# First column of x: half of it loaded in two parts by two queues, the first weights' high part made by VectorE, and two products put ahead of the second half's transposes

## What is computed

```python
h = rmsnorm(x, g_pre_mix)
proj = h @ w_in + b_in                     # 18 tiles of 128 columns
out_a = mixer_a(...)                       # sliding window, 8 query heads, 2 key heads
out_b = mixer_b(...)                       # chunked attention, 8 heads
x = x + rmsnorm(concat(out_a, out_b) @ w_out, g_post_mix)
u = square(relu(rmsnorm(x, g_pre_mlp) @ w_up))      # 1024 x 4096
x = x + rmsnorm(u @ w_down, g_post_mlp)
```

## Time and profile before

| | us |
|---|---|
| median of three runs | 1034.25 |
| the profiled execution | 1034.96 |
| its span, first to last instruction | 1032.9 |
| TensorE busy in the span | 1024.1 (99%) |
| VectorE | 771.6 (75%) |
| ScalarE | 470.1 (46%) |
| GpSimd | 220.3 (21%) |

### The profile page before, as it was taken

How to read it: one execution, slowest core, us unless ns; L and a number is a source line. 1 busy time by engine, 2 the same in 40 slices (tenths; PEclk the granted TensorE clock), 3 DMA queues, 4 the chain that set the end, 5 groups by cost and what they waited for, 6 DMA issues and landing times.

```text
span 1032.9 us, 15795 instructions
## 1 busy us (share of the span) xinstructions
PE 1024.1 (99%) x5525; PEld 852.3 (83%) x5525; DVE 771.6 (75%) x1507; ACT 470.1 (46%) x977; POOL 220.3 (21%) x218
## 2 busy tenths in 40 slices
PE   9999999999999999999999999999999999999997
PEld 8899887788777888888888888888888888888886
DVE  4955677766688478888988788786444777778997
ACT  6622355545478567836221221311344445454552
POOL 5200000000000003148675674771100000000000
PEclk9999999999999999999999999999999999999999
DMA  9935442110071474035444434446777733454344
GB/s 196 225 100 135 108 133 76 44 47 27 21 224 43 123 185 157 25 138 209 168 170 162 163 133 153 163 143 217 252 237 243 233 101 94 142 194 142 94 139 166
DMA packets 135070, 147.91 MB, mean 143 GB/s; under 512 B 72248, under 2 KB 85440, under 8 KB 132944
## 3 DMA queue, kind: packets, MB, share of 16 engines
q1 hardware_dynamic: 133920, 146.68, 45.7%
q10 hardware_dynamic: 688, 0.20, 0.1%
q0 software_dynamic: 384, 0.04, 0.1%
HBM read 103.65 MB, written 47.49 MB: 146 GB/s over the span
## 4 chain that ended last, share of the span: by engine, by line
PE 93%; DVE 3%; issue 2%; DMA 1%; ACT 1%; POOL 0%; DVEq 0%; SPq 0%; ACTq 0%
PE ps L2246 27%; PE ps L2248 27%; PE ps L2247 27%; PE ps L2469 3%; PE ps L2455 3%; PE ps L2436 2%; PE ps L2380 1%; DVE wc_lo L1922 1%; PE ps L2415 1%; PE ps L2590 1%; PE ps L2588 1%; PE ps L2576 1%; DMA up_raw<-in_w_up 1%; DVE b_lo L1911 1%; DMA xraw<-in_x 0%
## 5 line engine op out<-in xcount | busy, mean ns | idle before, releaser
L2246 PE MATMUL ps<-b_hi,wc_hi 128*128 128x512 f32 x448 | 174.8, 390 | 0.5 <-DVE wc_lo L1922 0.5
L2246 PE MATMUL ps<-tm_hi,sm_hi 128*128 128x512 f32 (+1 forms) x450 | 174.9, 389 | 0.0
L2247 PE MATMUL ps<-tm_lo,sm_hi 128*128 128x512 f32 (+1 forms) x450 | 174.8, 389 | 0.0
L2248 PE MATMUL ps<-tm_hi,sm_lo 128*128 128x512 f32 (+1 forms) x450 | 174.8, 389 | 0.0
L2247 PE MATMUL ps<-b_lo,wc_hi 128*128 128x512 f32 x448 | 174.5, 390 | 0.0
L2248 PE MATMUL ps<-b_hi,wc_lo 128*128 128x512 f32 x448 | 174.5, 390 | 0.0
L1484 ACT ACTIVATE sm_hi<-sm_raw 128x512 fp32r<-128x512 f32 x112 | 70.7, 631 | 163.0 <-DMA sm_raw<-u_matrices 163.0
L2150 DVE TENSOR_TENSOR sm_lo<-sm_raw,sm_hi 128x512 fp32r<-128x512 f32 x112 | 77.9, 695 | 78.1 <-ACT sm_hi L1484 77.4
L2246 PEld LDWEIGHTS ps<-b_hi,wc_hi 128*128 128x128 f32 x448 | 84.2, 188 | 18.4 <-DVE wc_lo L1922 0.9
L2248 PEld LDWEIGHTS ps<-tm_hi,sm_lo 128*128 128x128 f32 x450 | 84.5, 188 | 17.5
L2246 PEld LDWEIGHTS ps<-tm_hi,sm_hi 128*128 128x128 f32 x450 | 84.5, 188 | 17.3
(11 more groups left out here) (261 smaller groups left out, 2066.6 us busy)
## 6 DMA issues: line engine op xcount, KB each, us to landing
u_matrices<-stage SPq DMA_DIRECT2D x112, 256.0 KB, 2.0
sm_raw<-u_matrices SPq DMA_DIRECT2D x112, 256.0 KB, 2.6
up_raw<-in_w_up SPq DMA_DIRECT2D x16, 1024.0 KB, 5.0
w<-in_w_down SPq DMA_DIRECT2D x64, 256.0 KB, 3.8
w_raw<-in_w_in SPq DMA_DIRECT2D x8, 512.0 KB, 3.6
xr<-in_x SPq DMA_DIRECT2D x8, 512.0 KB, 4.5
x_rows<-xr SPq DMA_DIRECT2D x8, 512.0 KB, 4.8
xf<-x_rows SPq DMA_DIRECT2D x8, 512.0 KB, 3.6
```

Of the source, the lines that this page charges most:

```text
L2246: pe.matmul(out, w_hi_, x_hi_, start=start, stop=False)
L2247: pe.matmul(out, w_hi_, x_lo_, start=False, stop=False)
L2248: return pe.matmul(out, w_lo_, x_hi_, start=False, stop=stop)
```

## The change

What it does, part by part:

1. The first half of column 0 is loaded by two DMAs: SyncE loads tokens 0 to 255 in the place of the old load, and ScalarE loads tokens 256 to 511 ahead of its three weight loads. Both add to `s_in[0]`, so the waits for that semaphore ask for 32 instead of 16.
2. VectorE makes w1_hi of column 0, with a copy ahead of everything else it does for the columns; ScalarE no longer does.
3. TensorE multiplies ones six times instead of seven.
4. TensorE's order becomes: transposes of the first half, three turns, the products e = 2 and e = 1 of the first half, the transposes of the second half (with their wait for `s_x0`), product e = 0, and on as before.

```diff
@@ load_x
-                    sp.dma_start(xraw[:, 0, 0:4], src[:, 0:4]).then_inc(s_in[0], 16)
+                    sp.dma_start(xraw[:, 0, 0:2], src[:, 0:2]).then_inc(s_in[0], 16)
                     sp.dma_start(g1, g_pre_mix).then_inc(s_g1, 16)
                     sp.dma_start(xraw[:, 0, 4:8], src[:, 4:8]).then_inc(s_x0, 16)
@@ scalar
+            act.dma_start(xraw[:, 0, 2:4], x[2 * P:4 * P, 0:P].rearrange("(t p) n -> p t n", p=P)).then_inc(s_in[0], 16)
             load_first_weights(act, 0)
...
-                        act.wait_ge(s_in[k], 16)
+                        act.wait_ge(s_in[k], 16 if k else 32)
...
-                        if k == 0 and h == 0:
-                            first_hi(0)
@@ vector
+            dve.wait_ge(s_w1[0], 48)
+            nc.vector.tensor_copy(w1_hi[:, 0], w1_raw[:, 0]).then_inc(s_w1hi, 1)
             dve.wait_ge(s_g1, 16)
@@ tensor
+            def first_transposes(h):
+                pe.wait_ge(*((s_x0, 16) if h else (s_in[0], 32)))
+                for t in range(h * (T // 2), (h + 1) * (T // 2)):
+                    last = pe.transpose(two(0)[:, t * P:(t + 1) * P], xraw[:, 0, t], ident[:])
+                last.then_inc(s_xt, 1)
...
-            keep_awake(7)
+            keep_awake(6)
             pe.wait_ge(s_id, 3)
-            x_transposes(0)
-
+            first_transposes(0)
+            turns(3)
             pe.wait_ge(s_xhi, 1)
             pe.wait_ge(s_w1hi, 1)
             for e in (2, 1, 0):
                 if e == 0:
+                    first_transposes(1)
                     pe.wait_ge(s_xlo, 1)
```

More of the change, by code:

```diff
@@ L1199, in wo_high @@
             def wo_high(k):
-                act.wait_ge(s_in[k], (64 if k in EXCHANGED else 16) + (32 if k < 4 else 16))
+                act.wait_ge(s_in[k], (64 if k in EXCHANGED else 16 if k else 32) + (32 if k < 4 else 16))
                 nc.scalar.activation(wo_hi[:, k], wo_raw[:, k], ACT.Copy).then_inc(s_wohi, 1)
@@ L2254, in x_transposes @@
                 for t in range(T):
[L2255 to L2258, removed]
+                    last = pe.transpose(two(6)[:, t * P:(t + 1) * P], xraw[:, k, t], ident[:])
                     if k < 2 and t == T // 2 - 1:
```

## The result

| | before | after |
|---|---|---|
| median of 6 runs, us | 1034.53 (1034.15 to 1034.73) | 1037.9 (1036.75 to 1038.98) |
| profiled execution | 1034.96 | 1038.98 |
| its span | 1032.9 | 1037.2 |

The ratio is 1.0035, with a 95% interval of 1.0024 to 1.0046: slower by some 3.5 us, where I had forecast 1034.2 and no change that can be told. The result lies outside my range of 1033.6 to 1035.9. The runs also lie further apart, over 2.2 us in place of 0.6. The profiled execution of the changed kernel is the slowest of its six, so what its trace shows is a bad case of the loss and not the middle one.

The account below looks back on a forecast made before the run. TensorE, busy 99% of the span, was taken as the bound; 1034.96 less a 0.1 us gain gives 1034.86, and the median lying 0.71 us below that execution gives 1034.15, rounded 1034.2; range 1033.6 to 1035.9.

Parts of the forecast that it names:

- the weights' high part: Column 0's w_hi on VectorE: third weight load lands at 5.28, copy ready for TensorE at 5.85, at no cost.
- the weights land last: Rival: weights landing at 6.4 hold the first products until 6.97; 0.47 us lost, 1034.7; chance 0.12.
- The clock: Rival at TensorE's start: gaps delay the rise past 7.13, up to 2.4 us lost (1036.6), around 1035.5 if partial; chance 0.18.
- The two rivals: Late weights before the first products (0.47 us, chance 0.12) and a later clock rise (up to 2.4 us, chance 0.18).
- the forecast gain: At product e = 0 of column 0: start at 7.36 instead of 7.44, a gain of 0.1 us.
- One pair of ones fewer: At TensorE's start: frees it 0.49 us earlier, at 3.71 instead of 4.20; no gain by itself.
- The order: Two products before the second half's transposes: same 1.71 us of lower-level work before e = 0, waits in between met.
- Transposes at 3.94: First half's transposes on TensorE were to start at 3.90 instead of 4.29, just behind the landing.
- the half landed: First half of column 0, loaded in two parts: 3.1 us to landing, at 3.85 instead of 4.16.
- the copy: VectorE's w_hi copy of 384 elements in SBUF: 0.42 us, ending at 5.75.
- product e = 0: Last first-half product of column 0 on TensorE: start at 7.36, with bounds of 7.29 or 7.56.

Follow-up runs that it names:

- e6: The changed kernel with SyncE holding back column 1 and all later loads until the first weights have landed; 1036.53 us in one run.
- e2: The changed kernel without the load in two parts: the first half is one SyncE load again; 1034.38 us.
- e11: The changed kernel with the second half's transposes put back ahead of all products; 1036.47 us.
- e1: The kernel before with only the load of the first half in two parts added; 1036.27 us.
- e8: The changed kernel with one weight load moved to SyncE's queue, ahead of g1 and the second half, and six turns instead of three; 1034.74 us.
- e8b: The same kernel as e8, run again for its comparison with the kernel before; 1034.78 us.
- e5: The kernel before without the multiplications of ones and the three turns, whose results are unused; 1036.41 us.
- e9: The kernel of e8 with the second half's transposes ahead of all products, as in the kernel before; 1034.6 us.
- e10: The kernel of e2 with seven pairs of ones instead of six and five turns instead of three; 1034.65 us.
- e7: The changed kernel with its weight loads reordered, the two in 256-byte pieces first and the one in 512-byte pieces last; 1037.02 us.

## Why the prediction was wrong

**The step that failed is the weights' high part**, and in it the duration of the third weight load. I took 3.1 us for it, from the row of the kernel before, and bounded it by 2.5 and 4.24. Both bounds came from loads issued before column 1's 512 KB. The load took 5.45 us in the profile, and 4.3 to 5.45 in the four profiled executions that have the change's loads. The issue moved by 0.6 us (to 2.30, forecast 2.18), the landing by 2.3 us more than that, and the first product by 2.4 us against the forecast (8.28 for 5.88). e6 points to the cause that was left out of the bound: at 2.30 the load is issued behind column 1's 512 KB (2.24), and with those and the later loads held back it takes 3.5 us, in one execution. The rival "the weights land last" named the mechanism, with a price of 0.47 us from a bound that was too near and a chance of 0.12.

**The clock was priced as if it stood by itself.** I had it rise later because of small gaps, 0.18, for 1.5 to 2.4 us. The small gaps alone did little to the median: e2 has them and differs from the kernel before by 0.3 us, inside its interval. In the profile of the change the clock had already risen, by 4.4 us, and fell in the gap of 3.39 us that the late weights make. The length of the gaps alone does not tell: the clock also fell in e11, after gaps of 0.81 and 0.92 us, and stayed up in e1, after 1.14 and 0.47 us. The two rivals came together: wait 1.8 us, clock 2.7 us in the profiled execution. A bound on the first should have carried the price of the second.

The moment at which the clock rose before was read a little wrong as well. I let a first product at the lower level take 0.43 us. In the change, at a granted clock of 0.50, the first one takes 0.56 us to the second (8.28 to 8.84), and only the next ones 0.43. By that the clock rose at about 7.0, not at 7.13, and the forecast gain would have been 0.14 us in place of 0.1. One pair of ones fewer shortened their row by 0.43 us (3.36 to 2.93), not 0.49, as 14 matmuls have 13 spaces and not 12. Neither matters beside the weights.

**The order.** That w_hi is no longer covered by the transposes was said, at no cost. The cost can appear once the weights are late: the second half's transposes leave the wait, which is then one gap of 3.39 us instead of two shorter ones, and come after it, at the lower level (9.27 to 9.98). The profile of e2 shows this cost, 1.89 us at column 1 together with the late clock. The difference between e11 and the change, about 1.4 us, fits it, but its interval is too wide to call the share shown.

**What held.** Transposes at 3.94 (forecast 3.90); the half landed at 0.76 + 3.0 = 3.76 (3.85); the copy took 0.36 us (0.42); what TensorE lost at the head went through to the end of the span almost whole (4.3 of 4.54). The lower level doubles the spacing: the lo x hi products of the change stand 0.43 apart (three from 10.55 to 11.83), 0.23 at the upper level. In e8 and e8b, where the weights are in time, product e = 0 started at 7.21 and 6.93, for my 7.36, both helped by a clock that rose earlier, by the spacing at about 6.7 and before 4.3. That a view of the granted clock without an entry doesn't mean full speed was read rightly from the spacing: e5's products at 7 us are 0.45 apart where the same column says 1.00 for its 7 to 10 us stage.

On loads that several engines issue, the Trainium skill says in "DMA: Bandwidth & Descriptors", Issuing engines are not separate DMA queues, that they interleave on the same 16 DMA engines and that only the time to issue is saved. The trace agrees in part. The half of x came 0.4 us sooner all the same (3.76 for 4.16), while the last weight load behind it landed about 2.9 us later (7.75 for 4.8). I had weighed the sharing for x but not for the weights.

## What to carry to other kernels

A load put at the head of a queue is charged to the last load of that queue, and its price must be worked out with all the traffic that will be under way when that one is issued, not with its old duration. Ask what the engine that waits for it will do meanwhile: in the profiled execution the wait for the weights cost 1.8 us and the clock that fell meanwhile 2.7 us more. Work that covers a landing of unsure time is worth leaving there even where the profile shows it a little late.

## What the runs showed that I had not expected

The same three weight loads land at very different times from one execution to the next: with the change's lists the last took 4.3, 5.0, 5.0 and 5.4 us in four executions, with those of e8 3.7, 3.7 and 4.2 (e9), and in the old lists 3.1 (before), 3.5 (e5), 3.6 (e10) and 4.5 us (e2). The kernel before has room for this, since it needs w_hi only at 6.78. The clock's rise varies as well: by the spacing it was at about 7 in the profile of before, ahead of 4.5 in those of the change, of e1 and of e8b, and at about 10 in those of e2, e5 and e7. In e2 and e7 the granted clock reads 1.00 throughout that stretch, so only the spacing shows it. Why the medians of e8 and e8b don't gain the 0.2 to 0.4 us that their profiled executions show at the head is open; no run tells the landings or the clock of the executions that weren't profiled.
